# Silus of a head loop regrouped from five groups to four, and the last quarter of the decay output gated one head later

## Chip, cores and metric

The kernel runs on one core of one Trainium2 chip. The metric is the device time of one execution in microseconds (us): the median of several executions, smaller is better. Three executions of the kernel before are shown, and one more that the hardware profiler recorded.

## What is computed

A first block (short convolution, mixture of experts, latent attention, mixture of experts, over 272 tokens of width 1024) is followed by a second block of two layers over 256 tokens. The change touches only the second block, in both of its layers. Each layer there is, cut to what matters:

```python
h = rmsnorm_2(x, pre_norm[layer])
proj = h @ w_in[layer]
(hq, hf, hi, hz, nq, kc, vc, ks, vs, kw, vw, ng, nz) = jnp.split(proj, offsets, axis=-1)
o_h = hgrn2_mixer(heads(hq), heads(hf), heads(hi), lower_bounds)
o_h = rmsnorm_2(o_h, hgrn_out_norm[layer]).reshape(B, S, HGRN_WIDTH) * jax.nn.silu(hz)
o_n = nsa_mixer(heads(nq), ...)
o_n = o_n.reshape(B, S, NSA_WIDTH) * jax.nn.silu(nz)
y = jnp.concatenate([o_h, o_n], axis=-1).astype(x.dtype) @ w_out[layer]
x = x + rmsnorm_2(y, post_norm[layer]).astype(x.dtype)
```

`o_h`, 1024 features by 256 tokens, is the output of the decaying recurrence ("decay output"); `o_n` is that of the sparse attention with 8 heads of 128 features. Each is multiplied by a Silu of its own gate, `hz` or `nz`, before the output projection `w_out`.

## The kernel before, in words

Five engines run one instruction list each and meet at semaphores. The lists are written out by hand, so the place of a step in an engine's list decides when it can run. Features lie on the 128 partitions and tokens along the free axis: a tile of 128 features by 256 tokens is 128x256, and a "unit" of projected weights gives two such tiles.

**Exact products.** The projections use fp32r products in three passes (`mm3`, L454 to L456): the upper part of weight and input, then the two mixed ones. Each operand must therefore be split first. The upper part is a rounding copy on ScalarE (ACT, L1013); the lower part is a subtraction on VectorE (DVE, L1393 for weights) or on GpSimd (POOL, `lower`, L1339, for gated outputs). Weights arrive through SyncE's DMA queue (SP, `load_dense`, L386) in a ring of three pairs of slots: the load of a unit waits for the last product that used the unit three before it.

**The head loop.** After the recurrence and the projections that precede it, each layer runs a loop over 8 attention heads h on every engine.

- TensorE (PE, L935 to L962): half a tile pair of one gate projection (`beside(h, 0)`), four transposes for each of two branches into banks 4 and 5 (L942 to L945), the scores of head h + 2, then `beside(h, 1)`, and last the six products of head h with the values. For h from 0 to 5 `beside` makes one unit of `IN_HEADS`, in the order NZ1, HZ1, NZ2, HZ2, HZ3, NZ3 (a unit of gates `nz` or `hz` serves a quarter of the features). At h = 6 and 7 its second half is the first and second unit of the output projection on `o_h` (`part_out(u, ...)` with source 0). Ahead of the first, at h = 6, PE waits for all four quarters of the split decay output: `t.next(b2["oh_lo"], 4)`, L930.
- ScalarE (L1291 to L1313): takes over the first projected tile (`land`, which first makes the upper part of a weight unit fetched ahead), copies the transposed bank 4 (L1296, L1297), the exponentials of head h + 2 (L1273), the second projected tile, then at the heads named in `GATED` the Silus of the units named there (`gate`, L1264). At h = 6 and 7 it next makes the upper part of one weight unit of the output projection (`upper`, L1305; the unit of h = 6 is the one that takes the slot of NZ3). Then, at the heads in `HGRN_AT`, it waits for DVE's gated quarter (`o_h`) and makes its upper part (L1311). Last it waits for head h's attention output (`o_n`) and makes its upper part (L1313). Before h = 0's end NZ0 and HZ0 are gated too (L1303).
- VectorE (L1882 to L1900): at the heads in `HGRN_AT` it waits for the Silu of quarter u (`gated`, L1889) and multiplies the quarter, 128x512 (L1891); then it copies bank 5 (L1893, L1894), scales the probabilities of h + 1 (`probs`), takes the maxima of h + 2, makes a weight unit's lower part (two halves of 128x1024, L1393), and multiplies head h's product with its gate (`output`, L1869).
- GpSimd (L1354 to L1361): at the heads in `HGRN_AT` the lower part of the gated quarter, 128x512; at every head the lower part of the attention output, 128x256.

After the loop PE runs two more units on `o_h` and four on `o_n` (L964 to L972), and a norm ends the layer.

The two tables that the change edits are `GATED` and `HGRN_AT` at L99 and L100. A Silu and an exponential need different function tables on ScalarE; where they alternate, the profile shows an `ACT_TABLE_LOAD` at the line of the function that needs it.

Of the kernel before, what the change touches and what calls it, by code (L numbers as in the profile page):

```python
# [95 lines left out]
SPLIT_AT = {0: (1, 1), 1: (1, 1), 2: (1, 1), 3: (1, 1), 4: (0, 1), 5: (0, 1), 6: (1, 1), 7: (0, 1)}  # L96
BEFORE_HEADS = [("unit", U_NZ), ("unit", U_HZ)]
IN_HEADS = [("unit", u) for u in (U_NZ + 1, U_HZ + 1, U_NZ + 2, U_HZ + 2, U_HZ + 3, U_NZ + 3)]
GATED = {1: (0, 1), 3: (2, 3), 4: (4,), 5: (5,)}  # L99
HGRN_AT = {1: 0, 2: 1, 4: 2, 5: 3}  # L100
MAKES = FIRST + [m for job in JOBS for m in job] + BEFORE_HEADS + IN_HEADS


# [77 lines left out]
def build(nc, h_in, consts_in, vecs_in, dense, experts, out):  # L181
    with ExitStack() as ctx:
# [38 lines left out]
        def V(name, of=vecs):  # L221
            a, n = VEC_AT[name]
            return of[:, a:a + n]
# [137 lines left out]
        def wide(v):  # L361

            return v.rearrange("p a b -> p (a b)")
# [631 lines left out]
        def _(act):  # L995
# [16 lines left out]
            def copy(o, i):  # L1012
                return act.activation(o, i, ACT.Copy)  # L1013
# [3 lines left out]
            def upper(last):  # L1017

                while to_split and to_split[0] <= last:
                    slot, _, count = PLAN[to_split.pop(0)]  # L1020
                    act.wait_ge(landed[slot], count)
                    copy(ring_parts[:, PAIRS_OF_SLOTS + slot, :], ring[:, slot, :]).then_inc(w_hi, 1)
# [198 lines left out]
            def layer2(layer):  # L1221
# [37 lines left out]
                def gate(units):  # L1259

                    for _, u in units:
                        act.wait_ge(b2["pj_copied"], LAYER_TILES * layer + MADE["unit", u])
                        x = wide(b_p[:, UNITS_2[u][1]:UNITS_2[u][1] + 2, :])
                        act.activation(x, x, ACT.Silu).then_inc(b2["z_ready"], 1)  # L1264
# [26 lines left out]
                for h in range(HEADS):  # L1291
# [12 lines left out]
                    if h >= len(IN_HEADS):  # L1304
                        upper(FIRST_2 + L2_UNITS * layer + LAST_FETCHED + h - len(IN_HEADS) + 2)  # L1305
                    if h in GATED:
                        gate([IN_HEADS[n] for n in GATED[h]])
                    if h in HGRN_AT:
                        t.next(b2["o_h"])
                        at = HGRN_AT[h]  # L1310
                        copy(b_ohs[0][:, 2 * at:2 * at + 2, :], b_p[:, F_HZ + 2 * at:F_HZ + 2 * at + 2, :]).then_inc(b2["oh_hi"], 1)  # L1311
# [22 lines left out]
        def _(gp):  # L1334
            t = Turns(gp)

            def lower(lo, whole, hi):

                return gp.tensor_tensor(lo, whole, hi, ALU.subtract)  # L1339

            def layer2(layer):
# [12 lines left out]
                for h in range(HEADS):  # L1354
                    if h in HGRN_AT:
                        t.next(b2["oh_hi"])
                        at = slice(2 * HGRN_AT[h], 2 * HGRN_AT[h] + 2)
                        lower(b_ohs[1][:, at, :], b_p[:, F_HZ + at.start:F_HZ + at.stop, :], b_ohs[0][:, at, :])\
# [22 lines left out]
        def _(v):  # L1381
# [36 lines left out]
            def stt(o, a, s, b, op1, op2, sem=None):  # L1418
                t.link(v.scalar_tensor_tensor(o, a, s, b, op1, op2), sem)
# [266 lines left out]
            def layer2(layer):  # L1686
# [174 lines left out]
                def gated(u):  # L1861

                    v.wait_ge(b2["z_ready"], 8 * layer + (BEFORE_HEADS + IN_HEADS).index(("unit", u)) + 1)
# [18 lines left out]
                for h in range(HEADS):  # L1882
                    pt = n_pt[h % 2]
                    if h == 0:
                        t.next(b2["oroot"])
                        stt(wide(b_ke), wide(b_ke), V(f"on{layer}"), wide(b_qe), ALU.mult, ALU.mult)
                    if h in HGRN_AT:
                        u = HGRN_AT[h]
                        gated(U_HZ + u)  # L1889
# [159 lines left out]
```

## Time and profile before

| | |
|---|---|
| median of three executions | 1980.35 us |
| lowest, highest | 1977.47, 1987.95 us |
| the profiled execution, its own time | 1975.22 us |
| its span from first to last instruction | 1973.1 us |
| what lies around the span | 2.12 us |
| mean granted TensorE clock | 0.929 of full speed |
| busy: PE, PE weight load, DVE, ACT, POOL | 88%, 64%, 44%, 32%, 3% |
| head loop of layer 0 | about 1486 to 1567 us of the span |
| head loop of layer 1 | about 1845 to 1925 us |

A row of a timeline gives start, duration, engine, line, operation, output and inputs, the count of instructions that were merged (x2), and in brackets the idle time of the engine before it with what ended that. Where a group is merged, its duration is that of the group. Matmuls are pipelined: one is shown with 0.28 us while the next starts 0.12 us later, so the spacing counts and not the duration.

### The profile page before, as it was taken

How to read it: one execution, taken by the hardware profiler on the slowest of the kernel's cores; microseconds unless marked ns; L12 is line 12 of the kernel's file. 1: busy time of each engine (PE TensorE's matmuls, PEld its weight loads, DVE VectorE, ACT ScalarE, POOL GpSimd, SP SyncE). 2: the span in 40 equal slices, each digit the busy share in tenths (PEclk: the TensorE clock that was granted, in tenths of full speed). 3: DMA queues.
4: the chain of work that ended last, by engine and by line, in shares of the span. 5: the costliest groups of instructions: out<-in, count | busy, mean ns of one | idle time of the engine just before them, and what ended most of it. 6: DMA issues, size and time to landing. Idle time of an engine off the chain costs nothing.

```text
span 1973.1 us, 31286 instructions
## 1 busy us (share of the span) xinstructions
PE 1740.4 (88%) x12626; PEld 1268.3 (64%) x12626; DVE 868.8 (44%) x1532; ACT 629.0 (32%) x1021; POOL 50.5 (3%) x54
## 2 busy tenths in 40 slices
PE   7999778888788899988787887989999988999997
PEld 7985334334336778443343442789888978998897
DVE  5742112122126644221221221668876564888554
ACT  4422111111014542111111111454447554453763
POOL 0200000000000010000000000000001100000010
PEclk9989988889889989988988989989999998999999
DMA  7638999999997313999999999434522334343222
GB/s 299 231 149 369 421 421 422 421 422 421 422 421 303 106 43 150 406 421 421 422 421 422 421 421 421 158 127 137 197 86 95 108 107 147 131 171 107 94 100 106
DMA packets 73089, 526.34 MB, mean 267 GB/s; under 512 B 8240, under 2 KB 8496, under 8 KB 9264
## 3 DMA queue, kind: packets, MB, share of 16 engines
q1 hardware_dynamic: 73008, 525.18, 66.7%
q8 instruction: 61, 1.00, 0.2%
q14 instruction: 20, 0.16, 0.0%
HBM read 524.10 MB, written 1.05 MB: 266 GB/s over the span
## 4 chain that ended last, share of the span: by engine, by line
PE 49%; DMA 27%; DVE 10%; SPq 7%; ACT 4%; issue 2%; POOL 0%; DVEq 0%; ACTq 0%
DMA arena<-experts 19%; PE banks L450 12%; PE banks L454 9%; PE banks L455 8%; PE banks L456 8%; SPq L409 7%; DMA ring<-experts 5%; PE banks L609 4%; DMA ring<-dense 3%; PE banks L594 3%; PE banks L627 3%; DVE arena L1413 2%; DVE ring_parts L1393 2%; ACT ring_parts L1013 1%; DVE hT L1544 1%
## 5 line engine op out<-in xcount | busy, mean ns | idle before, releaser
L454 PE MATMUL banks<-arena_parts,ring_parts 128*128 128x256 f32 (+1 forms) x1444 | 429.0, 297 | 41.6 <-DVE arena_parts L1408 15.3
L456 PE MATMUL banks<-arena_parts,ring_parts 128*128 128x256 f32 (+1 forms) x1444 | 417.8, 289 | 0.0
L455 PE MATMUL banks<-arena_parts,ring_parts 128*128 128x256 f32 (+1 forms) x1444 | 417.7, 289 | 0.0
L450 PEld LDWEIGHTS banks<-arena 128*128 128x128 f32 (+3 forms) x2704 | 340.4, 199 | 76.4 <-issue 60.5
L450 PE MATMUL banks<-arena 128*128 128x128 f32 (+5 forms) x2704 | 375.6, 296 | 13.3 <-DVE arena L1539 5.0
L454 PEld LDWEIGHTS banks<-arena_parts,ring_parts 128*128 128x128 f32 x1444 | 281.8, 195 | 52.4 <-issue 19.5
L1013 ACT ACTIVATE arena<-banks 128x256 f32<-128x256 f32 (+9 forms) x350 | 160.0, 485 | 477.7 <-PE banks L450 204.8
L1393 DVE TENSOR_TENSOR ring_parts<-ring,ring_parts 128x1024 fp32r<-128x1024 f32 x208 | 248.4, 1238 | 119.1 <-ACT ring_parts L1013 117.4
L609 PE MATMUL banks<-ring,arena 128*32 128x512 f32 x1536 | 214.4, 668 | 93.8 <-DMA ring<-experts 90.8
L455 PEld LDWEIGHTS banks<-arena_parts,ring_parts 128*128 128x128 f32 x1444 | 283.1, 196 | 0.2
L456 PEld LDWEIGHTS banks<-arena_parts,ring_parts 128*128 128x128 f32 x1444 | 282.1, 195 | 0.0
L1013 ACT ACTIVATE ring_parts<-ring 128x2048 fp32r<-128x2048 f32 x104 | 198.7, 1913 | 204.6 <-DMA ring<-dense 204.6
L609 PEld LDWEIGHTS banks<-ring,arena 128*32 128x32 f32 x1536 | 41.7, 114 | 245.1 <-DMA ring<-experts 186.2
L1572 DVE TENSOR_TENSOR arena<-arena,banks 128x256 f32<-128x256 f32 x32 | 13.5, 421 | 390.7 <-ACT arena L1086 390.7
L594 PE MATMUL banks<-arena 128*128 128x272 f32 x544 | 157.8, 413 | 13.8 <-DVE hT L1544 4.5
L1086 ACT ACTIVATE arena<-banks 128x256 f32<-128x256 f32 x32 | 12.3, 384 | 436.9 <-PE banks L609 436.9
L609 PE MATMUL banks<-arena 128*32 128x512 f32 x512 | 98.7, 862 | 46.3 <-DMA arena<-experts 46.3
L1544 DVE TENSOR_TENSOR hT<-hT,banks 128x272 f32<-128x272 f32 x272 | 116.6, 437 | 49.6 <-PE banks L594 45.7
L594 PEld LDWEIGHTS banks<-arena 128*128 128x128 f32 x544 | 86.4, 188 | 75.8 <-DVE hT L1544 66.5
L609 PEld LDWEIGHTS banks<-arena 128*32 128x32 f32 x512 | 12.7, 128 | 133.4 <-DMA arena<-experts 128.6
L627 PE MATMUL banks<-arena 128*32 128x512 f32 x768 | 89.0, 596 | 0.0
L1574 DVE COPY arena<-banks 128x256 f32<-128x256 f32 x32 | 13.6, 425 | 167.4 <-PE banks L615 167.4
(207 smaller groups left out, 1609.4 us busy)
## 6 DMA issues: line engine op xcount, KB each, us to landing
ring<-experts SPq DMA_DIRECT2D x192, 1024.0 KB, 26.2
arena<-experts SPq DMA_DIRECT2D x160, 1024.0 KB, 20.8
ring<-dense SPq DMA_DIRECT2D x112, 1024.0 KB, 4.9
at<-experts SPq DMA_DIRECT2D x32, 1024.0 KB, 22.9
consts<-consts_in SPq DMA_DIRECT2D x1, 1414.0 KB, 13.7
vecs<-vecs_in SPq DMA_DIRECT2D x1, 1125.5 KB, 15.9
hT<-h_in SPq DMA_DIRECT2D x2, 544.0 KB, 4.3
out<-x SPq DMA_DIRECT2D x4, 256.0 KB, 2.3
```

Source lines behind the costliest of these rows:

```text
L409: sp.dma_start(expert_slot(u), experts[layer, (i + 1) % QUADS, u]).then_inc(m[f"landed{u}"], 16)
L450: return pe.matmul(o, lhsT, rhs, start=(k == 0), stop=(k == n - 1))
L454: pe.matmul(o, lhsT[0], rhs[0], start=(k == 0), stop=False)
L455: pe.matmul(o, lhsT[0], rhs[1], start=False, stop=False)
L456: return pe.matmul(o, lhsT[1], rhs[0], start=False, stop=(k == n - 1))
L594: pe.matmul(psum[:, 6 + c % 2, 0:T], mo_y[:, c * P:c * P + P], mo_sw[:, 0:T], start=True, stop=True).then_inc(s["cmb_done"], 1)
L609: m = pe.matmul(psum[32 * e:32 * e + 32, 3, :], mo_xs[:, k, 32 * e:32 * e + 32], w[:, e, :], start=(k == 0), stop=(k == 7), tile_position= ...
L627: m = pe.matmul(psum[32 * e:32 * e + 32, 4 + half, :], mo_ht[:, k, 32 * e:32 * e + 32], w[:, e, :], start=(k == 0), stop=(k == 1), tile_po ...
L1013: return act.activation(o, i, ACT.Copy)
L1393: v.tensor_tensor(ring_parts[:, slot, at], ring[:, slot, at], ring_parts[:, PAIRS_OF_SLOTS + slot, at], ALU.subtract).then_inc(w_ready, 1)
L1413: t.link(v.tensor_tensor(o, a, b, op), sem)
L1544: v.tensor_tensor(hT[:, c, :], hT[:, c, :], psum[:, 6 + c % 2, 0:T], ALU.add).then_inc(s["add_done"], 1)
```

## The change

```diff
-GATED = {1: (0, 1), 3: (2, 3), 4: (4,), 5: (5,)}
-HGRN_AT = {1: 0, 2: 1, 4: 2, 5: 3}
+GATED = {1: (0, 1), 3: (2, 3), 5: (4, 5)}
+HGRN_AT = {1: 0, 2: 1, 4: 2, 6: 3}
```

The keys of `GATED` are heads, its values indexes into `IN_HEADS`: 4 is HZ3 and 5 is NZ3. The keys of `HGRN_AT` are heads, its values quarters of the decay output. Both tables are read in both layers. The Silu of HZ3 moves from head 4 to head 5 on ScalarE. The product of quarter 3 with it (VectorE), its upper part (ScalarE) and its lower part (GpSimd) move from head 5 to head 6. Nothing in PE's or SP's list changes.

## Rows read from the trace of the kernel before

**Rows 1.** The first page, busy times of the engines over the whole span.
```profile
PE 1740.4 (88%) x12626; PEld 1268.3 (64%) x12626; DVE 868.8 (44%) x1532; ACT 629.0 (32%) x1021; POOL 50.5 (3%) x54
```

**Rows 2.** Busy times by stretch: bounds, length, PE, PEld, DVE, ACT, POOL, granted clock, DMA share, GB/s.
```profile
1850.00:1906.10 56.10, 56.10 (x429) 52.07 (x427) 36.35 (x78) 45.06 (x100) 7.94 (x8) 1.00 0.31 104
1906.10:1908.00 1.90, 0.04 (x1) 0.00 (x0) 1.72 (x4) 1.38 (x5) 1.28 (x2) 1.00 0.65 272
1908.00:1962.00 54.00, 53.97 (x432) 52.55 (x432) 20.09 (x20) 19.29 (x28) 2.74 (x3) 1.00 0.28 98
...
1549.30:1602.00 52.70, 52.65 (x421) 51.84 (x422) 22.45 (x23) 19.75 (x24) 6.36 (x6) 0.97 0.41 140
```

**Rows 3.** Timeline of PE where head 6 begins `part_out(0)`: layer 0, then layer 1.
```profile
1549.35 0.58 PE L454 MATMUL banks<-arena_parts,ring_parts 128*128 128x256 f32 x1 [1.90 <-POOL arena_parts L1339]
...
1908.03 0.39 PE L454 MATMUL banks<-arena_parts,ring_parts 128*128 128x256 f32 x1 [1.90 <-POOL arena_parts L1339]
```

**Rows 4.** Timeline of ACT in layer 1, from head 4's Silu to head 6's weight copy.
```profile
1895.07 0.63 ACT L1264 ACTIVATE arena<-arena 128x512 f32<-128x512 f32 x1
...
1900.21 1.28 ACT L1273 ACT_TABLE_LOAD   x1
1902.18 0.37 ACT L1273 ACTIVATE arena<-banks,arena 128x128 f32<-128x128 f32 x1 [0.69 <-DVE arena L1416]
...
1904.20 1.28 ACT L1264 ACT_TABLE_LOAD   x1
1905.49 0.63 ACT L1264 ACTIVATE arena<-arena 128x512 f32<-128x512 f32 x1
1906.03 0.92 ACT L1013 ACTIVATE arena_parts<-arena 128x512 fp32r<-128x512 f32 x2
1906.85 0.62 ACT L1013 ACTIVATE arena<-banks 128x384 f32<-128x384 f32 x2
1908.02 1.92 ACT L1013 ACTIVATE ring_parts<-ring 128x2048 fp32r<-128x2048 f32 x1 [0.54 <-DMA ring<-dense]
```

**Rows 5.** Timeline of POOL in layer 1: heads 5 (two instructions) and 7.
```profile
1906.72 1.95 POOL L1339 TENSOR_TENSOR arena_parts<-arena,arena_parts 128x512 fp32r<-128x512 f32 x2 [8.39 <-ACT arena_parts L1013]
1916.93 0.73 POOL L1339 TENSOR_TENSOR arena_parts<-arena,arena_parts 128x256 fp32r<-128x256 f32 x1 [8.26 <-ACT arena_parts L1013]
1925.60 1.33 POOL L1339 TENSOR_TENSOR arena_parts<-arena,arena_parts 128x256 fp32r<-128x256 f32 x1 [7.94 <-ACT arena_parts L1013]
```

**Rows 6.** Timeline of DVE in layer 1, heads 5 to 7.
```profile
1895.80 0.69 DVE L1413 TENSOR_TENSOR arena<-arena 128x512 f32<-128x512 f32 x1 [0.66 <-ACT arena L1264]
...
1906.24 0.56 DVE L1893 COPY arena<-banks 128x384 f32<-128x384 f32 x1 [0.67 <-PE banks L945]
...
1907.10 0.90 DVE L1413 TENSOR_TENSOR arena<-arena,vecs 128x4 f32<-128x4 f32 x1
...
1909.59 2.36 DVE L1393 TENSOR_TENSOR ring_parts<-ring,ring_parts 128x1024 fp32r<-128x1024 f32 x2
...
1925.11 2.91 DVE L1393 TENSOR_TENSOR ring_parts<-ring,ring_parts 128x1024 fp32r<-128x1024 f32 x2
```

**Rows 7.** Timeline of ACT in layer 0: head 5's copies, head 6's weight copy.
```profile
1547.34 0.92 ACT L1013 ACTIVATE arena_parts<-arena 128x512 fp32r<-128x512 f32 x2
...
1549.63 1.91 ACT L1013 ACTIVATE ring_parts<-ring 128x2048 fp32r<-128x2048 f32 x1 [0.84 <-DMA ring<-dense]
```

**Rows 8.** Timeline of PE: two restarts after idle times of about 4 us.
```profile
1320.42 0.58 PE L454 MATMUL banks<-arena_parts,ring_parts 128*128 128x256 f32 x1 [4.13 <-DVE ring_parts L1393]
...
1618.37 0.55 PE L454 MATMUL banks<-arena_parts,ring_parts 128*128 128x256 f32 x1 [3.94 <-DVE arena_parts L1408]
```

**Rows 9.** By stretch, columns of rows 2: what followed the restarts of rows 3 and 8.
```profile
1320.40:1323.40 3.00, 2.98 (x14) 2.98 (x15) 3.00 (x3) 1.91 (x1) 0.00 (x0) 0.50 0.03 8
1549.30:1552.40 3.10, 3.05 (x14) 3.06 (x15) 3.03 (x5) 1.91 (x1) 0.67 (x1) 0.50 0.00 0
1618.40:1624.00 5.60, 5.60 (x24) 5.47 (x25) 4.63 (x13) 3.78 (x7) 0.00 (x0) 0.50 0.00 0
...
1908.00:1911.00 3.00, 2.97 (x25) 2.97 (x26) 2.93 (x4) 1.92 (x1) 0.67 (x1) 1.00 0.02 5
```

## The prediction

> **What bounds the kernel now.** I read the first page, then the busy times by stretch around the two head loops, then the timelines of PE, ACT, POOL and DVE there. The page gives PE 88% of the span and ACT 32% [rows 1]; that is an average over stages, so it only says where to look. The stretches say more. In layer 1, from the head loop's start to the transposes of head 6, PE is busy for 56.10 of 56.10 us; then comes one hole of 1.90 us; after it PE is busy for 53.97 of 54.00 us, up to the norm that ends the layer [rows 2]. Layer 0 has the same hole, and 52.65 of 52.70 us behind it [rows 2]. So PE sets the pace on both sides, and whatever makes that hole longer is paid in full: nothing downstream waits for anything but PE.
>
> The hole has a name. In both layers PE stands 1.90 us ahead of the first product of the output projection, released by GpSimd's subtraction [rows 3]. That is L930, the wait for all four quarters of the split decay output. What comes before it in layer 1 is a chain with hardly a gap [rows 4, 5]: exponentials of head 7 (1902.18), table load (1904.20, 1.28 us), Silu of NZ3 (1905.49, 0.63 us), upper part of quarter 3 (first of the two copies at 1906.03), lower part on GpSimd (first of the two at 1906.72), PE at 1908.03. From the start of that upper copy to PE it is 2.00 us; in layer 0 it is 1549.35 - 1547.34 = 2.01 us [rows 3, 7].
>
> **The change, part by part.**
>
> *Silu of HZ3 from head 4 to head 5.* Head 4 loses a Silu (0.63 us) and the table load before it; head 5 loses the load that brings the exponentials back (1900.21, 1.28 us), and gains the 0.63 us [rows 4]. ACT is relieved of two loads in each layer, 4 x 1.28 = 5.1 us of its time in all. I cost this at nothing. At heads 4 and 5 PE has no idle time that a faster ACT could remove [rows 2], and the exponentials of head 7 were not waiting for the table: after the load ended at 1901.49 ACT stood 0.69 us for DVE's maxima [rows 4]. They start at 1902.18 as before, and the Silu load at 1904.20 too. If PE's cover were gone, the relief would be worth up to the 5.1 us.
> The Trainium skill's page "ScalarE: Activation LUTs" (section "What ACT_TABLE_LOAD costs") puts a switch at about 2.66 us, load and drain together; here the trace disagrees, since the Silu starts 0.01 us after its load ends. By the page four switches would be 10.6 us of ACT's time, equally covered.
>
> *Product of quarter 3 from head 5 to head 6 on DVE.* It costs 0.69 us and followed its Silu by 0.10 us [rows 4, 6]. DVE reaches head 6 at about 1905.57, 0.67 us before its bank copy at 1906.24 [rows 6]. The HZ3 Silu is now first at 1905.49 and ends at 1906.12, so the product runs from 1906.22 to 1906.91, and DVE's bank copy slips from 1906.24 to 1906.95, 0.7 us. Behind it are the probabilities of head 7 and a weight unit's lower part; PE wants both only after `part_out(0)`, which takes over 5 us. That slip costs nothing by itself.
>
> *Upper part from head 5 to head 6 on ACT.* Here is the cost. In head 6's list three things stand before it: the copies of bank 4, the upper part of a weight unit, and the wait for DVE's product. The bank copies end near 1907.5 as before, since one Silu more and one 128x512 copy less about cancel. The weight copy starts at 1908.02, when its DMA has landed, and takes 1.92 us [rows 4]. That landing cannot move forward, for its slot is freed by PE's last product of NZ3, which is untouched. Back to back on ACT, the next instruction starts about 0.1 us before the shown end (0.63 us Silu, next start 0.54 us later [rows 4]), so the upper part of quarter 3 starts at about 1909.84 instead of 1906.03: 3.81 us later. In layer 0 the weight copy starts at 1549.63, so the upper part starts at 1551.45 instead of 1547.34: 4.11 us later [rows 7]. Together 7.9 us, all of it ahead of PE's wait, which holds up everything behind it in PE's list: `part_out(0)`, head 6's value products, head 7. SP's queue waits in turn for `part_out(0)` to free a slot, so it moves along by the same amount.
>
> *Lower part on GpSimd.* Before, it ran 1906.72 to about 1907.99 for 128x512 [rows 5]. It began 0.69 us after the upper part did, so it will now be ready at about 1909.84 + 0.69 = 1910.53, while DVE works at a weight unit's lower part in two halves of 1.2 us, shown from 1909.59 to 1911.95 before [rows 6]. The two disturb each other. DVE's product of 128x4 at 1907.10 took 0.90 us and ended just when GpSimd's first subtraction did [rows 5, 6]; a 128x256 subtraction takes 0.73 us alone and 1.33 us at 1925.60, where DVE's pair began at 1925.11 and took 2.91 instead of 2.36 us [rows 5, 6]. So GpSimd waits for the half in progress: between nothing (it arrives between halves) and 1.2 us (it has just missed one). DVE's pair starts between 1909.1 (if the stretches of the small products fall away) and 1910.3 (before, plus 0.7), so the rest of a half that meets GpSimd is mostly 0.4 to 1.0 us. I take 0.55 us in each layer, 1.1 us, the extra of the nearest row (1.33 - 0.73 = 0.6); range 0 to 2.4.
> The Trainium skill's page "SBUF — State Buffer" (section "SBUF: two separate sides") calls this an exclusive lock held for a whole instruction, between a GpSimd operation and a DVE one with two inputs in SBUF. The rows bear it out, and it speaks against the change.
>
> *Clock.* PE's hole grows from 1.90 to 1.9 + 3.8 or 4.1 + 0.55, some 6.3 to 6.6 us. After 4.13 and 3.94 us of idling PE ran at 0.50 of full clock (1.2 GHz) for 3.0 and 5.6 us [rows 8, 9]. At that level 14 matmuls take 3.05 us, against 25 in 2.97 us at full clock (2.4 GHz) [rows 9]. With 0.119 us each at full clock, the half-speed stretches lost 2.98 - 14 x 0.119 = 1.3 us and 5.60 - 24 x 0.119 = 2.7 us. The 1.90 us hole cost 1.4 us in layer 0 and nothing in layer 1 [rows 9], so a short hole has an even chance of it and pays 0.7 us on average; the long one surely pays, 1.3 to 2.7 us, say 1.8. Extra: between 1.3 x 2 - 1.4 = 1.2 and 2.7 x 2 - 1.4 = 4.0 us against this execution; I take 2.0.
>
> **Sum.** 3.8 + 4.1 + 1.1 + 2.0 = 11.0 us. The profiled execution had 1975.2 us (span 1973.1 and 2.1 around it) and would become 1986.2. It lies 5.1 us below the median of the three executions and below their lowest, so the predicted median is 1980.35 + 11.0 = 1991.4 us, +0.56%.
>
> **Rivals.**
>
> *Small: only the order on ACT counts.* The clock falls no more often than now (or the executions timed mostly had both drops already, so nothing is new), and GpSimd slips in between DVE's halves. Then +7.9 to 9.8 us, about 1989.3, within 0.5%. For it: a 1.90 us hole already brought a drop in layer 0. Against it: the two 4 us holes brought longer half-speed stretches. Chance 0.31.
>
> *Large: the long hole costs two spells of half clock.* After 1618.37 half speed lasted 5.6 us of work [rows 9]. If both layers get that, and GpSimd misses a half each time, it is 7.9 + 2.4 + 4.0 = 14.3 us, 1994.7. It is the end of the forecast's case rather than another mechanism; chance 0.15.
>
> *Faster: ACT's table loads decide.* The chain into PE's hole runs over ACT, with a table load in it. In this kernel the mechanism would be that the relief at heads 4 and 5 pulls head 6 forward, enough to remove the holes: 2 x 1.90 plus the 1.4 us of clock in layer 0, 5.2 us, 1975.2 us. It decides from the point where the exponentials of head 7 can start 1.9 us sooner and the upper part of quarter 3 no longer queues behind the weight copy. Against it: ACT stood 0.69 us for DVE, and a list runs in order. Chance 0.03. By the page "ScalarE: Activation LUTs" of the Trainium skill (section "Table sets: the hidden batching unit") all work of one table set should be done before a switch, which is where this change goes.
>
> *It does nothing: the added delay is absorbed.* PE would have to find idle time behind the hole to give back; there is 0.03 us in 54.00 and 0.05 in 52.70 [rows 2]. Chance 0.03, about 1980.4 us.
>
> **How the numbers follow.** The forecast has 0.48, of which most is over 0.5%, the large case 0.15, the small case 0.31, absorbed 0.03, faster 0.03. A measurement of this kernel can tell about 0.5% from no change, here 9.9 us, and my 11.0 lies close to that line. Slower by over 0.5%: the large case and 0.46 of the forecast, 0.61; within 0.5%: 0.36; faster: 0.03. The range begins at the small case with its bare 7.9 us, less the 2.9 us by which the lowest of the three executions lies under their median: 1980.35 + 7.9 - 2.9 = 1985.4. It ends at the large case and half of that spread: 1994.7 + 1.4 = 1996.1.
>
> **What would show it.** In the changed profile: PE's idle ahead of `part_out(0)` about 6.3 us in both layers, still released by GpSimd L1339; on ACT the order weight copy (released by the DMA), then 128x512 upper part at once; GpSimd's 128x512 subtraction shown longer than 1.27 us, beside a DVE weight pair; eight table loads at the Silus instead of ten, six at the exponentials instead of eight in the two loops; half clock right after the hole in both layers; PE gapless on both sides. Wrong, if the hole keeps 1.90 us (then ACT's order is not what delays it), if DVE's product is late instead, or if idle time appears in the tail that swallows the difference.

## The result, and the profile after

The changed kernel is slower: 1994.49 us (median of six executions, 1991.17 to 1999.3) against 1981.62 us (six executions of the kernel before). The ratio is 1.006, 95% interval 1.0039 to 1.0081. Forecast were 1991.4 us, a range of 1985.4 to 1996.1, and "slower by over 0.5%" with a chance of 0.61.

The first page shows the load of the engines nearly unchanged; ACT has four instructions fewer, the four table loads:

```profile
PE 1753.2 (88%) x12626; PEld 1279.5 (64%) x12626; DVE 866.4 (43%) x1532; ACT 623.8 (31%) x1017; POOL 51.8 (3%) x54
```

The lines of the Silu (L1264) and of the exponentials (L1273) have eight and six table loads, for ten and eight before:

```profile
L1264 ACT ACT_TABLE_LOAD  x8: 1283/1283/1283, 1503.8 to 1921.1; - x8
...
L1273 ACT ACT_TABLE_LOAD  x6: 1283/1283/1283, 1510.2 to 1906.7; - x6
```

The timeline of PE at the start of `part_out(0)`, layer 0 and layer 1, answers to [rows 3]. PE's idle time ahead of it, the hole, was 1.90 us in each layer and is now 6.47:

```profile
1564.17 0.58 PE L454 MATMUL banks<-arena_parts,ring_parts 128*128 128x256 f32 x1 [6.47 <-POOL arena_parts L1339]
...
1929.52 0.58 PE L454 MATMUL banks<-arena_parts,ring_parts 128*128 128x256 f32 x1 [6.47 <-POOL arena_parts L1339]
```

By stretch (columns of [rows 2]): PE is busy up to the hole and busy behind it, in both layers, but each restart has some 6 us at half clock (0.50 in the column of the granted clock).

```profile
1499.50:1557.60 58.10, 58.10 (x444) 54.14 (x444) 37.62 (x83) 42.34 (x99) 7.92 (x8) 1.00 0.30 100
1557.70:1564.10 6.40, 0.00 (x0) 0.00 (x0) 5.07 (x9) 3.77 (x6) 2.63 (x2) 0.68 0.19 81
1564.10:1567.00 2.90, 2.83 (x13) 2.83 (x14) 0.00 (x0) 0.00 (x0) 0.02 (x1) 0.50 0.00 0
1567.00:1570.00 3.00, 3.00 (x16) 3.00 (x16) 0.00 (x0) 0.00 (x0) 0.00 (x0) 0.50 0.00 0
...
1572.00:1618.00 46.00, 46.00 (x379) 45.21 (x379) 18.56 (x18) 17.63 (x23) 5.70 (x5) 1.00 0.47 160
...
1923.00:1929.50 6.50, 0.05 (x1) 0.00 (x0) 5.07 (x9) 3.82 (x7) 2.69 (x2) 0.67 0.19 82
1929.50:1932.50 3.00, 2.98 (x14) 2.98 (x15) 0.00 (x0) 0.00 (x0) 0.00 (x0) 0.50 0.02 5
1932.50:1935.50 3.00, 3.00 (x16) 3.00 (x16) 0.00 (x0) 0.00 (x0) 0.00 (x0) 0.51 0.00 0
```

The timeline of ACT in layer 1 answers to [rows 4]. The two Silus stand together; then come the copies of bank 4, the weight copy released by its DMA, and only then the 128x512 upper part of quarter 3:

```profile
1921.11 1.28 ACT L1264 ACT_TABLE_LOAD   x1
1922.41 1.15 ACT L1264 ACTIVATE arena<-arena 128x512 f32<-128x512 f32 x2
1923.46 0.40 ACT L1013 ACTIVATE arena_parts<-arena 128x256 fp32r<-128x256 f32 x1
1923.77 0.62 ACT L1013 ACTIVATE arena<-banks 128x384 f32<-128x384 f32 x2
1925.00 1.91 ACT L1013 ACTIVATE ring_parts<-ring 128x2048 fp32r<-128x2048 f32 x1 [0.60 <-DMA ring<-dense]
1926.81 0.61 ACT L1013 ACTIVATE arena_parts<-arena 128x512 fp32r<-128x512 f32 x1
```

GpSimd's subtraction of quarter 3 and, by the timeline of VectorE, the product of quarter 3 and the weight pair (two subtractions, merged in one row) that ran beside GpSimd [rows 5, 6]:

```profile
1927.50 1.97 POOL L1339 TENSOR_TENSOR arena_parts<-arena,arena_parts 128x512 fp32r<-128x512 f32 x1 [2.83 <-ACT arena_parts L1013]
```
```profile
1923.14 0.69 DVE L1413 TENSOR_TENSOR arena<-arena 128x512 f32<-128x512 f32 x1 [0.65 <-ACT arena L1264]
...
1925.99 2.36 DVE L1393 TENSOR_TENSOR ring_parts<-ring,ring_parts 128x1024 fp32r<-128x1024 f32 x2
```

**Where the time went.** The profiled execution took 1999.30 us, 24.1 us more than the profiled one before, though the medians differ by 12.9. Anchors on PE split it. Each head loop has one product that waits about 1.2 us for ACT in head 0 (before at 1489.22 and 1847.92, after at 1499.48 and 1864.83); layer 1 starts its products at 1618.37 and 1634.58. From head 0's anchor of layer 0 to layer 1's first product it is 129.15 us before and 135.10 after; from layer 1's anchor to the end of the span, 125.18 and 132.37. These two stretches, called the loop stretches below, hold 254.33 us before and 267.47 after: +13.1 us, close to the difference of the medians, 12.9. The rest, 10.3 us ahead of the first anchor and 0.7 between, lies where nothing was changed. Over the twelve profiles of this study the first anchor falls anywhere from 1489.2 to 1502.1 us, and latest in one of the fastest kernels (run 4), so I take it for scatter between executions; run 7 tests it. So the loop stretches are the finer measure, and each run below is read by them beside its timed ratio.

### The profile page after: what moved, and what is told of

It is laid out like the page before. It is cut to its first block, busy times and chain, and to the rows that moved or that the text cites. A ratio compares the mean times of both kernels' runs of the same rounds, so it can differ in the third digit from the quotient of the medians.

```text
span 1997.2 us, 31282 instructions
## 1 busy us (share of the span) xinstructions
PE 1753.2 (88%) x12626; PEld 1279.5 (64%) x12626; DVE 866.4 (43%) x1532; ACT 623.8 (31%) x1017; POOL 51.8 (3%) x54
## 4 chain that ended last, share of the span: by engine, by line
PE 49%; DMA 30%; DVE 9%; SPq 7%; ACT 4%; issue 2%; POOL 0%; DVEq 0%; ACTq 0%
DMA arena<-experts 20%; PE banks L450 12%; PE banks L454 9%; PE banks L456 9%; PE banks L455 9%; DMA ring<-experts 7%; SPq L409 6%; PE banks L609 3%; DMA ring<-dense 3%; PE banks L594 2%; PE banks L627 2%; DVE arena L1413 2%; DVE ring_parts L1393 2%; ACT ring_parts L1013 1%; DVE hT L1544 1%
## 5 line engine op out<-in xcount | busy, mean ns | idle before, releaser
L450 PEld LDWEIGHTS banks<-arena 128*128 128x128 f32 (+3 forms) x2704 | 346.7, 202 | 78.6 <-issue 62.9
L450 PE MATMUL banks<-arena 128*128 128x128 f32 (+5 forms) x2704 | 384.1, 300 | 13.0 <-DVE arena L1539 5.0
```

What stands on the lines that cost most here:

```text
L450: return pe.matmul(o, lhsT, rhs, start=(k == 0), stop=(k == n - 1))
```

## The experiments

Each timed ratio is against the kernel before on the same chip.

**1. ACT's order in head 6.** The changed kernel, with the upper part of quarter 3 made ahead of the weight unit's (in all diffs here, lines are left out at `...`):

```diff
-                    if h >= len(IN_HEADS):
-                        upper(FIRST_2 + L2_UNITS * layer + LAST_FETCHED + h - len(IN_HEADS) + 2)
                     if h in GATED:
...
                     if h in HGRN_AT:
...
+                    if h >= len(IN_HEADS):
+                        upper(FIRST_2 + L2_UNITS * layer + LAST_FETCHED + h - len(IN_HEADS) + 2)
```

> The changed kernel, but in head 6 ScalarE makes the upper part of quarter 3 ahead of the weight unit's upper part instead of behind it. My theory (the delay is ScalarE's order in head 6): the upper part starts when the bank copies end, some 2.5 us sooner than in the changed kernel, and GpSimd's subtraction with it; PE's hole ahead of part_out(0) falls from 6.5 us to 3.3 to 3.9 us in both layers, and the kernel gains 5 to 8 us on the changed one. Rival (the late product on VectorE or the late Silu holds the quarter): the hole stays at 6.5 us, since neither moves. Rival (the difference of the two kernels is noise or lies elsewhere): the hole shrinks and the time does not follow.

Measured: ratio 1.0025 (1.0009 to 1.0041), 1987.0 us against 1982.55. The timeline of PE, layer 0 and layer 1:

```profile
1551.62 0.58 PE L454 MATMUL banks<-arena_parts,ring_parts 128*128 128x256 f32 x1 [3.51 <-POOL arena_parts L1339]
...
1915.60 0.58 PE L454 MATMUL banks<-arena_parts,ring_parts 128*128 128x256 f32 x1 [3.50 <-POOL arena_parts L1339]
```

The hole falls by 3.0 us in each layer, though product and Silu are as late as in the changed kernel. The loop stretches are 6.5 us over those of the kernel before, instead of 13.1. One reordered copy takes back half of the loss: the wait behind the weight copy is its largest piece, and the rival on VectorE falls.

**2. The late quarter alone.** The kernel before with `GATED` as it was:

```diff
-HGRN_AT = {1: 0, 2: 1, 4: 2, 5: 3}
+HGRN_AT = {1: 0, 2: 1, 4: 2, 6: 3}
```

> One half of the change alone: quarter 3 is gated in head 6, but the Silus stay in five groups. My theory: the whole loss is here, hole of 6.3 to 6.5 us in both layers as in the changed kernel, +11 to +14 us on the kernel before. Rival (the bigger Silu group of head 5 makes the quarter late): hole near 1.9 us, time of the kernel before. If the two table loads per layer that are back cost anything, it would be slower than the changed kernel by up to 5 us; I expect no difference.

Measured: ratio 1.005 (1.0033 to 1.0067), 1991.06 us against 1982.55; holes of 5.88 and 5.84 us; loop stretches +10.1 us. Most of the loss is here. The hole is 0.6 us shorter than I expected, and the timelines of POOL and VectorE say why:

```profile
1923.37 1.36 POOL L1339 TENSOR_TENSOR arena_parts<-arena,arena_parts 128x512 fp32r<-128x512 f32 x1 [3.34 <-ACT arena_parts L1013]
```
```profile
1918.40 0.69 DVE L1413 TENSOR_TENSOR arena<-arena 128x512 f32<-128x512 f32 x1
...
1921.24 2.36 DVE L1393 TENSOR_TENSOR ring_parts<-ring,ring_parts 128x1024 fp32r<-128x1024 f32 x2
```

With the Silu of HZ3 already done in head 4, VectorE multiplies at once (no idle time before 1918.40, where the changed kernel has 0.65 us). Its weight pair is then over at 1923.60, 0.23 us after GpSimd could start. In the changed kernel the pair ends at 1928.35, 0.85 us after. So the regrouping has a small price of its own inside the change, about 0.6 us of hole per layer. The other 1.8 of the 3.0 us between the two kernels' stretches go with shorter spells of half clock, 3.5 us behind each restart against some 6 (last section); no run separates them.

**3. The four groups alone.** The kernel before with the changed `GATED`; VectorE's product of quarter 3 moves to the end of head 5:

```diff
-GATED = {1: (0, 1), 3: (2, 3), 4: (4,), 5: (5,)}
+GATED = {1: (0, 1), 3: (2, 3), 5: (4, 5)}
...
                     lower_next(1)
                     output(h)
+                    if h == 5:
+                        hgrn(HGRN_AT[h])
```

> The other half alone: Silus in four groups, quarter 3 still gated in head 5 on every engine. VectorE's product has to stand at the end of head 5 there, behind output(5), since ahead of the bank copy it would wait for a Silu that waits for it. My theory: the upper part starts behind two Silus and the product, 0.8 to 0.9 us later than before, so the hole is 2.7 to 3.2 us in both layers (1.9 before), +2 to +5 us on the kernel before with the clock. Rival (saved table loads make the loop faster): hole at or under 1.9 us, time 2 to 5 us under the kernel before.

Measured: ratio 1.0001 (0.9979 to 1.0024), 1982.67 us against 1982.55; holes of 2.84 us in both layers; loop stretches +4.6 us. The timed ratio can't tell that from nothing, since its interval reaches to +0.24%, 4.8 us. The hole is as expected, 0.94 us longer than before. The rival wanted a hole of at most 1.9 us: two loads less per layer did not shorten it.

**4. The upper part early.** The kernel before, five groups, with ACT making quarter 3's upper part where its input is ready:

```diff
                     copy(pt[0:NCMP, 0, 3 * P:4 * P], ...)
+                    if h == 5:
+                        quarter(HGRN_AT[h])
                     if h + 2 < HEADS:
                         exps(h + 2)
...
-                    if h in HGRN_AT:
+                    if h in HGRN_AT and h != 5:
```

(`quarter` is the wait for `o_h` with the copy behind it, L1309 to L1311.)

> The kernel before (five groups, quarter 3 in head 5), but ScalarE makes quarter 3's upper part ahead of the exponentials of head 7, where its input is already done, instead of behind the Silu of NZ3. My theory: GpSimd's subtraction is done some 4 us before PE asks for it, the hole of 1.9 us goes in both layers (0 to 0.3 us left), exponentials of head 7 start no later than before (0.69 us of slack against a copy of 0.6), and the kernel is 4 to 6 us faster than before: 3.8 us of idling and some of the clock. Rival (something else is due at the same time, a weight unit's lower part or the bank copies): PE waits there instead and the time stays.

Measured: ratio 0.9956 (0.9941 to 0.9971), 1973.48 us against 1982.55. The timeline of ACT in head 5 of layer 1:

```profile
1910.45 0.61 ACT L1013 ACTIVATE arena_parts<-arena 128x512 fp32r<-128x512 f32 x1
1911.08 1.28 ACT L1273 ACT_TABLE_LOAD   x1
...
1912.49 0.37 ACT L1273 ACTIVATE arena<-banks,arena 128x128 f32<-128x128 f32 x1
```

and PE by stretch, from head 0 to the middle of head 6 and over the place where the hole was:

```profile
1858.00:1916.00 58.00, 57.94 (x443) 54.16 (x444) 38.55 (x84) 45.64 (x103) 9.22 (x9) 1.00 0.29 98
1916.00:1930.00 14.00, 14.00 (x116) 13.62 (x115) 7.95 (x13) 6.15 (x9) 1.48 (x2) 1.00 0.34 122
```

The hole is gone in both layers and nothing took its place. The copy fits into ACT's slack ahead of the exponentials; they start 54.43 us behind the anchor, 0.17 us later than before, and PE does not wait for them. Loop stretches -5.7 us: 3.8 us of holes, the 1.4 us of half clock in layer 0 [rows 9], and 0.5 us that I don't assign. The timed gain of 0.44% is 8.7 us, with an interval of 5.7 to 11.7; the stretches lie at its lower end.

**5. PE kept busy in the hole.** The changed kernel, with six products of 128x512 more at L930, whose result is overwritten:

```diff
                         if h == len(IN_HEADS):
+                            keep_clock(0, 6)
                             t.next(b2["oh_lo"], 4)
```

> The changed kernel, with six products of 128x512 into a free bank on PE ahead of its wait in head 6 (they compute nothing that is used). They take some 5 us of the 6.5 us hole, so the wait itself still ends when GpSimd is done. It measures the clock's share alone. Clock theory: PE restarts at full clock, the stretch from the end of the transposes to the end of the layer shortens by 1.4 to 2.8 us in each layer, 3 to 5 us in all on the changed kernel. Rival (the clock's share is small, the rest of the difference is elsewhere): under 1 us per layer. If the products run past GpSimd's end, the hole's end moves later and the gain is eaten.

Measured: ratio 1.0063 (1.0035 to 1.0091), 1994.15 us against 1980.55. By stretch, layer 1: the dummy products, what is left of the wait, and the restart.

```profile
1920.60:1925.70 5.10, 5.10 (x13) 1.98 (x11) 4.82 (x9) 3.82 (x7) 1.38 (x2) 1.00 0.25 103
1925.70:1927.10 1.40, 0.10 (x1) 0.00 (x0) 0.25 (x1) 0.00 (x0) 1.36 (x1) 1.00 0.00 0
1927.10:1930.00 2.90, 2.88 (x24) 2.88 (x25) 0.00 (x0) 0.00 (x0) 0.00 (x0) 1.00 0.00 0
```

The wait ends where it did (`part_out(0)` starts 64.69 us behind the anchor, in both layers, exactly as in the changed kernel), but PE restarts at full clock, 24 products in 2.88 us instead of 14 in 2.98. The loop stretches are 5.0 us shorter than in the changed kernel, 2.3 and 2.7. The timed median did not follow, so the same kernel was measured again (run 8).

**6. GpSimd and VectorE.** The changed kernel, with VectorE's weight pair of head 6 moved ahead of the product of quarter 3 (one profiled execution, no timed series):

```diff
+                    if h == 6:
+                        lower_next(1)
                     if h in HGRN_AT:
...
-                    lower_next(1)
+                    if h != 6:
+                        lower_next(1)
                     output(h)
```

> The changed kernel, with VectorE's pair of weight subtractions in head 6 moved to the head's front, so that it is over before GpSimd's 128x512 subtraction can start. Theory of the shared access: the subtraction takes 1.3 to 1.6 us instead of 1.9 to 2.0, and the hole is shorter by as much, 5.8 to 6.2 us instead of 6.5. Rival (GpSimd is slower for another reason, such as the DMA or ScalarE next to it): it stays at 1.9 to 2.0 us. The product of quarter 3 is made 1.7 us later, still before ScalarE wants it; if not, ScalarE's upper part starts late and the hole grows.

Measured: holes of 6.25 and 6.26 us; loop stretches +12.4. The timelines of POOL and VectorE:

```profile
1920.87 1.66 POOL L1339 TENSOR_TENSOR arena_parts<-arena,arena_parts 128x512 fp32r<-128x512 f32 x1 [2.13 <-ACT arena_parts L1013]
```
```profile
1920.73 0.68 DVE L1413 TENSOR_TENSOR arena<-arena 128x512 f32<-128x512 f32 x1
```

Shorter, 1.66 us for 1.97, but by less than expected: with the pair out of the way another VectorE product, 1920.73 to 1921.41, stood there. GpSimd ended 1.12 us after it. In the changed kernel it ended at 1929.47, 1.12 us after the pair, and in run 2 at 1924.73, 1.13 us after it. Three times the same: GpSimd finishes a fixed time after whichever two-input VectorE instruction it met. That fits a wait for the instruction in progress, and the rival (DMA or ScalarE beside it) gives no reason for a fixed distance. Run 1 shows both directions at once:

```profile
1914.06 1.49 POOL L1339 TENSOR_TENSOR arena_parts<-arena,arena_parts 128x512 fp32r<-128x512 f32 x1 [0.32 <-ACT arena_parts L1013]
```
```profile
1913.99 0.42 DVE L1878 TENSOR_TENSOR arena<-arena 128x256 f32<-128x256 f32 x1
1914.33 1.76 DVE L1413 TENSOR_TENSOR arena<-arena 128x512 f32<-128x512 f32 x1
```

GpSimd arrived during VectorE's 128x256 product and ended 1.14 us after it; VectorE's next product, 0.68 us in the other kernels, took 1.76 and ended 0.54 us after GpSimd. So whichever comes second pays.

**7 to 10. Once more, side by side on one chip.** First the changed kernel itself (7) and the busy hole (8):

> The changed kernel itself once more, as the yardstick for the next three on the same chip. Its profile before showed +13.1 us in the two layers and another +11 us of span upstream of the first head loop, where nothing was changed. If the upstream part is scatter between executions, the time is again 11 to 14 us over the kernel before and the holes are 6.2 to 6.5 us; if the change reached upstream, over 20 us.

> The busy hole once more, beside the changed kernel. Its profile gave 5 us back in the two layers, its timed median did not (1994.15 against 1994.49 us). If that was scatter, it is now 3 to 6 us faster than the changed kernel on the same chip; if the clock's share does not count in unprofiled executions, it is equal within 1 us.

Then the early upper part (9), and a version of it with four groups (10), where quarter 2 also moves from head 4 to head 5 (the loops over the quarters are adapted; only the tables are shown):

```diff
-GATED = {1: (0, 1), 3: (2, 3), 4: (4,), 5: (5,)}
-HGRN_AT = {1: 0, 2: 1, 4: 2, 5: 3}
+GATED = {1: (0, 1), 4: (2, 3, 4), 5: (5,)}
+HGRN_AT = {1: (0,), 2: (1,), 5: (2, 3)}
```

> Five groups with the early upper part once more: 5 to 9 us faster than the kernel before (its profile gave 5.7 us in the two layers, its timed median 9), no hole ahead of part_out(0) above 0.3 us.

> Four Silu groups without the late quarter: NZ2, HZ2 and HZ3 are gated together in head 4, NZ3 in head 5, quarters 2 and 3 both in head 5 with their upper parts early, as in the run before. It saves the same two table loads per layer as the change. My theory (loads are covered by PE, only the wait at L930 counts): no hole, the same time as with five groups within 2 us. Rival (fewer table loads are worth something): 3 to 5 us faster than with five groups. Rival (three Silus in a row make output(4) or the exponentials of head 7 late): a new wait on PE at head 5 or 6, slower.

| run | median, us | ratio to before (95%) | loop stretches against before, us |
|---|---|---|---|
| 7, changed kernel | 1994.78 | 1.0056 (1.0036 to 1.0076) | +13.3 |
| 8, busy hole | 1988.80 | 1.0034 (1.0018 to 1.005) | +7.7 |
| 9, early upper part | 1975.28 | 0.9958 (0.9941 to 0.9975) | -5.5 |
| 10, early, four groups | 1974.45 | 0.9971 (0.9956 to 0.9985) | -5.6 |

The kernel before had 1982.99 us. The changed kernel repeats: holes of 6.51 and 6.47 us, and a median 11.8 us over that of the kernel before, not over 20. Its profiled execution again has a first anchor 11 us late; run 4, the early version, has the latest, at 1502.1 us. So the time ahead of the loops is not the change's. The median of the busy hole is now 6.0 us under that of the changed kernel on the same chip, as its stretches say, though the two intervals overlap; run 5's median was scatter, as far as two series can tell. Run 10 has no hole either. The waits of PE from before the first head loop to the end (us in total, times, longest) have no entry for GpSimd any more, and none of the others is in heads 1 to 7:

```profile
PE banks L454 <- DVE ring_parts L1399: 6.3, 2, 4.1
PE banks L454 <- DVE arena_parts L1414: 3.9, 1, 3.9
PE banks L450 <- DVE arena L1419: 2.8, 3, 1.3
PE banks L454 <- ACT arena L1013: 2.5, 2, 1.3
PE banks L450 <- ACT arena L1000: 0.9, 1, 0.9
PE banks L454 <- ACT arena L1287: 0.7, 2, 0.4
```

It has eight and six table loads as the changed kernel has, for the ten and eight of run 9, and ties with run 9: the stretches differ by 0.1 us, where the rival wanted 3 to 5. The saved loads show no worth while PE covers them.

## Why the prediction was right, and where its sum was off

**The place and the order on ACT** held. Counted from the Silu load of head 5, the upper part starts 5.70 us later in layer 1 where it had been 1.83 (1921.11 to 1926.81, against 1904.20 to 1906.03 [rows 4]): 3.87 us. In layer 0 it is 3.92 us, less than the 4.1 forecast, since the weight unit landed 0.2 us sooner. Together 7.8 for 7.9. Run 1 showed the cause: the same copy ahead of the weight copy, and 3.0 of the 4.6 us that each hole had grown are gone.

**GpSimd's wait** was put at 0.55 us a layer and came to 0.70 and 0.65 us (1.97 and 1.92 us shown, 1.27 alone). The nearest row served well. The forecast said of VectorE's slip of 0.7 us that it "costs nothing by itself"; that was a little wrong. The slip is what lays the weight pair under GpSimd's subtraction: run 2, without most of it, has 1.26 and 1.36 us there. The cost itself was in the sum, as GpSimd's term.

**The holes** grew by 4.57 us each, 9.14 for 9.0 in the sum. All of it reached the end, as the forecast took from [rows 2]. Run 5, whose wait ends at the same place and which has no half clock behind it, is still 8.1 us over the kernel before in the stretches (run 8: 7.7), and 9.14 less the 1.4 us of clock that the kernel before lost [rows 9] is 7.7.

**The clock** is the term that was mis-sized: 2.0 us taken (its own 1.8 us a hole, less 1.4, gives 2.2), 4.0 measured (13.1 less 9.14), the upper end of its bounds. Both restarts had the long half-speed spell of about 6 us, where I had assumed a mean of a short and a long one. Run 5 gives the same by another way: without any half clock the stretches are 5.0 us shorter (5.6 in runs 7 and 8), of which 1.4 us were already lost before the change; that leaves 3.6 and 4.2 us for it. The large rival was right in that term and wrong in its other, two missed VectorE halves (2.4 us; the wait was 1.35). The small rival falls: the changed kernel lost clock in both layers in both of its profiles, where the profile before lost it in one.

**The table loads** went, 5.1 us of ACT's time, and gave nothing that a run can tell: run 3 is not faster than before, run 10 not faster than run 9. The rival that they decide falls. So does the one on absorption, since the longer holes reached the end.

The forecast median was 3.1 us under the measured one. About 2 us of that are clock, and 1.3 us the starting point (1980.35 where six executions give 1981.62). That the slowdown is over 0.5% is less certain than that it is there: the interval of the ratio begins at 0.39%, and the forecast's 11.0 us lay just as close to that line.

## What to carry to other kernels

Ask of a step that is moved down a hand-written list not what it costs but what now stands ahead of it on its engine, and who waits at its end: here a 0.6 us copy landed behind a 1.9 us copy that itself waits for a DMA, in front of the only wait of a gapless PE. Count table loads only where ScalarE is what the bound engine waits for. And once a profile names such a hole, the better edit may be the opposite one: making the same copy as soon as its input was there removed the hole and made the kernel 0.4% faster than before.

## What the runs showed of the hardware beyond expectation

How long PE stays at half clock does not follow from how long it stood. A hole of 6.47 us was followed by about 6 us of it in both layers; holes of 5.88 and 5.84 us (run 2) by some 3.5 us; holes of 3.51 and 3.50 us (run 1) by 4.6 and 5.9 us; and holes of 2.84 us (run 3) by nearly 6 us in layer 0 and 3 us in layer 1. The holes of 1.90 us before were followed by 3 us of it and by none [rows 9]. By stretch, run 3, layer 0 and then layer 1:

```profile
1554.20:1557.20 3.00, 2.97 (x14) 2.97 (x15) 2.93 (x4) 1.32 (x1) 0.67 (x1) 0.50 0.00 0
1557.20:1560.20 3.00, 3.00 (x16) 3.00 (x16) 0.95 (x1) 0.00 (x0) 0.00 (x0) 0.53 0.00 0
1915.50:1918.50 3.00, 2.94 (x14) 2.94 (x15) 2.93 (x5) 1.30 (x1) 0.70 (x2) 0.51 0.02 5
1918.50:1921.50 3.00, 3.00 (x27) 3.00 (x27) 0.98 (x1) 0.00 (x0) 0.00 (x0) 1.00 0.00 0
```

and run 1, layer 0, the spell and what follows it:

```profile
1551.60:1556.20 4.60, 4.58 (x21) 4.58 (x22) 2.88 (x3) 0.31 (x1) 0.00 (x0) 0.50 0.00 0
1556.30:1559.30 3.00, 3.00 (x27) 3.00 (x27) 0.00 (x0) 0.00 (x0) 0.00 (x0) 1.00 0.03 5
```

The price goes by the spell and not by the hole: 1.3 us for the 3 us of run 3's layer 1 and 2.6 for the 6 us of the changed kernel's (there the stretch grew by 7.2 us and the hole by 4.57), and for the 4.6 us here, at 0.119 us a product at full clock [rows 9], 4.60 - 21 x 0.119 = 2.1. So a hole of 2.8 to 6.5 us is better priced with a range, 1.3 to 2.6 us, than by its length; these runs do not say where in the range a hole will fall.
